# A hybrid mixer and MoE kernel: ten pieces of three weight blocks are loaded in the last tile of the RWKV recurrence

## The chip, the cores and the metric

The kernel runs on one core of a Trainium2 chip. The metric is the device time of one execution in microseconds (us). Times are medians of several runs; beside them stands one execution taken by the hardware profiler. The engines are TensorE (PE; its weight loads are listed as PEld), VectorE (DVE), ScalarE (ACT), GpSimd (POOL) and SyncE (SP), whose queue issues all the loads and stores here.

## The reference

One layer of a diffusion backbone over 256 latent tokens and 256 context tokens of width 1024. A modulated RMSNorm is followed by one input projection into three groups of heads: gated linear attention, RWKV-7 and Mamba-2 SSD. Each group is run in both directions, first over the context and then over the latent tokens from the context's last state. The three outputs are joined, projected and added to the input. Then comes a second modulated norm and a mixture of 32 experts, of which each token uses four:

```python
for e in range(N_EXPERTS):
    gu = t @ p['moe_w_gu'][e] + p['moe_b_gu'][e]
    glu, lin = jnp.split(gu, 2, axis=-1)
    glu = jnp.minimum(glu, SWIGLU_LIMIT)
    lin = jnp.clip(lin, -SWIGLU_LIMIT, SWIGLU_LIMIT)
    act = glu * jax.nn.sigmoid(SWIGLU_ALPHA * glu) * (lin + 1.0)
    y = y + gates[:, e:e + 1] * (act @ p['moe_w_down'][e] + p['moe_b_down'][e])
```

All is float32. The expert weights are 32 x 12 MB (12.6 million bytes each), by far the largest part of what is read.

## The kernel before

Everything on the chip lies in one SBUF arena of 57248 words per partition, and tensors of different stages share places in it. The stages are: modulation, norm and input projection with the GLA and SSD heads (to about 250 us of the profiled execution), the RWKV recurrence (to 367.5 us), the output projection, router and selection of tokens (to about 398 us), and the expert loop.

**Weight blocks and the ring.** An expert's weights are six blocks of 128 partitions x 4096 words (2.097 MB each): four of gate and up (s = 0 to 3) and two of down (s = 4, 5). They are read in order, expert by expert. The buffers are `ring[0]` to `ring[7]`; block number q of the whole sequence goes to ring q % 8, once TensorE has read the block that was in it (`ring_free[r]`, raised by TensorE after the last matmul on it). TensorE waits for `ring_full[r]`. Three further buffers, `ring[8]` to `ring[10]` (`RING`, `RING + 1`, `RING + 2`), are used once: they hold blocks 4, 5 and 3 of expert 20 (`AHEAD * GROUP`), loaded long before they are read. Two blocks, ring 4 (expert 0, block 4) and ring 6 (expert 1, block 0), lie where the output projection's weights and the residual stream are, and wait for these.

**The recurrence.** Four tiles of 128 tokens (s = 0 to 3), two directions each (d = 0, 1), in one chain through TensorE (`double`, `solve`, `transitions`, `updates`, `advance`, `outputs`), with DVE and ScalarE copying the products out of PSUM. Each tile has 6 doublings per direction, so there are 48 "rounds", named D{j}{s}{d}. Its working tensors (XT, Z, bt, AR, bm) have two halves, and tile s uses half s % 2. The third tile is s = 2 and so uses half 0; its last uses come in the first part of the last tile, s = 3, where TensorE's code has `solve(2)` (product qg2), `transitions(2)` (mt2), `updates(2)` (nv2) and later `outputs(2)` (ol2). The product `ro` ends the recurrence.

**Loads during the recurrence.** On the sync queue the loads are issued one part at a time (512 words per partition, 0.262 MB): `at_round(n)` makes the queue wait for round n's product, and `load_block_part(r, x)` issues part x of 8. In the last tile (rounds 36 to 47) these are the second half of ring 10 and the eight parts of ring 1 (issue line 681). The parts other than the eighth of a block raise `block_parts`, for which TensorE waits ahead of the expert loop (line 2977); the eighth raises `ring_full`. After `ro` the queue issues four whole blocks (`load_slot`, issue line 665): ring 3, 7, 8 and 9, which lie over the recurrence's working tensors; then the biases moe_b_gu (two rows of loads, line 716) and moe_b_down (line 717), which raise `late_in`, for which TensorE waits in `gates_by_expert`. Then come ring 4, ring 6, and from q = 8 on one block for each ring that comes free.

A semaphore table (`Rounds`) gives for each product the counts at which it is there (`Q.arrived`) and at which its PSUM bank has been read (`Q.emptied`).

Of the kernel before, what the change touches and what calls it, by code (L numbers as in the profile page):

```python
# [20 lines left out]
WORDS = 57248  # L21
RING = 8
PER = 6
GROUP = 4
AHEAD = 5
# [187 lines left out]
def rwkv_round_table():  # L213

    t = []

    def both(name, bank, parts=1):
        t.extend((f"{name}{d}", bank(d), parts) for d in (0, 1))

    doubling = lambda d: 2 * d  # L220
    lower, upper = (lambda d: 4 + 2 * d), (lambda d: 5 + 2 * d)

    def prepare(s, part):
        if part == 0:
            both(f"cu{s}", upper)
        if part == 1:
            both(f"ab{s}", lower)
        if part == 2:
            both(f"ak{s}", lower)
        if part == 3:  # L230
            both(f"bk{s}", lower)
            both(f"at{s}", upper)
        if part == 4:
            both(f"bv{s}", lower)

    def conclude(s, part):
        if part == 0:
            both(f"qg{s}", lower)
        if part == 1:
            both(f"mt{s}", lower)  # L240
        if part == 2:
            both(f"nv{s}", lower)
        if part == 3 and s > 0:
            both(f"rs{2 * s}", lower)
        if part == 4 and s < 3:
            both(f"rs{2 * s + 1}", lower)
        if part == 5 and s >= 2:
            both(f"ol{s}", lower)

    for part in range(4):  # L250
        prepare(0, part)
    for s in range(4):
        for j in range(DOUBLINGS):
            both(f"D{j}{s}", doubling, 2)
        if s < 3:
            prepare(s + 1, 0)
        prepare(s, 4)
        if s:
            for part in range(5):
                conclude(s - 1, part)  # L260
        if s < 3:
            prepare(s + 1, 1)
            prepare(s + 1, 2)
            prepare(s + 1, 3)
        else:
            conclude(2, 5)
    for part in (0, 1, 2, 3, 5):
        conclude(3, part)
    t.append(("ro", 0, 2))
    return t  # L270


def hybrid_block(nc, a):

    with ExitStack() as ctx:
# [109 lines left out]
        XT = [low.take(2, 4, 192) for _ in range(2)]  # L385
        XT = [XT[d].rearrange("p i (u m) (x t) -> p i u m x t", u=2, x=3) for d in range(2)]
        PLAIN, TURNED, SERIES = 0, 1, 2
        bm = [low.take(4, 64) for _ in range(2)]
# [15 lines left out]
        Z = [ra.take(8, 2, 64) for _ in range(2)]  # L404
        Z = [Z[d].rearrange("p (i o) x k -> p i o x k", i=2) for d in range(2)]
        bt = [ra.take(2, 2, 256) for _ in range(2)]
        AR = [ra.take(4, 2, 128) for _ in range(2)]
        AR = [AR[d].rearrange("p (i c) x (q t) -> p i c q x t", i=2, q=2) for d in range(2)]
# [4 lines left out]
        for x in (w0b, csil):  # L413
            room = over(x, 768)
            guarded, negative = room.take(2, 2, 65), room.take(2, P)
            d = len(eb)
# [51 lines left out]
        ring = [arena[:, ap.offset:ap.offset + 4096] for ap in ring_start] + held + [first_blocks[3]]  # L468
# [7 lines left out]
        Q = Rounds(rwkv_round_table(), bank_full, bank_free)  # L476
# [7 lines left out]
        ring_full = [sem(f"ring_full{r}") for r in range(RING + 3)]  # L484
# [14 lines left out]
        block_parts, out_parts = named("block_parts out_parts")  # L499
# [107 lines left out]
        gu_k = a["moe_w_gu"][0].rearrange("e (j p i) c -> e j p (i c)", p=P, i=2)  # L607
        dn_k = a["moe_w_down"][0].rearrange("e (j p i) c -> e j p (i c)", p=P, i=4)
# [12 lines left out]
        def extra_at(j, s):  # L621

            return s, j + (E * PER // RING - (1 if s in (3, 4, 5) else 0))
# [4 lines left out]
        def _(sp):  # L628
# [21 lines left out]
            for s, _, kind, n in loads[2 * KD + 2:]:  # L650
                if (kind, n) == ("in", 2):
                    sp.dma_start(Cb(1, C_N - 1), a["consts"][:, P:]).then_inc(consts_in, 16)
                if kind == "in":
                    size = KD * width_of(n)
                    slot_wait("in", n)
                    sp.dma_start(w_in_tile(n).rearrange("p k c -> p (k c)"), a["w_in"][w_in_at[n]:w_in_at[n] + P * size].rearrange("(p x) -> p x", p=P))\
                        .then_inc(slot_full[s], 16)
                elif kind == "ada":
                    load_ada(n)
            sp.dma_start(xT, a["xT"]).then_inc(xT_in, 16)  # L660

            def load_slot(r, e, s):

                src = gu_k[bass.ds(e, 1), s, :, :] if s < 4 else dn_k[bass.ds(e, 1), s - 4, :, :]
                sp.dma_start(ring[r], src.rearrange("a p c -> p (a c)")).then_inc(ring_full[r], 16)
# [7 lines left out]
            for n in range(2):  # L673
                s = place["out", n][0]
                slot_wait("out", n)
                sp.dma_start(slots[s], a["w_out"][n]).then_inc(slot_full[s], 16)
            def load_block_part(r, x):

                at = slice(512 * x, 512 * x + 512)
                src = gu_k[AHEAD * GROUP:AHEAD * GROUP + 1, 3, :, :] if r >= RING else gu_k[0:1, r, :, :] if r < 4 else dn_k[0:1, r - 4, :, :]  # L680
                sp.dma_start(ring[r][:, at], src.rearrange("a p c -> p (a c)")[:, at]).then_inc(ring_full[r] if x == 7 else block_parts, 16)

            def at_round(n):

                Q.arrived(sp, f"D{n % 12 // 2}{n // 12}{n % 2}")
# [16 lines left out]
            for x in range(8):  # L702
                at_round(28 + x)
                load_block_part(5, x)
            for x in range(4):
                at_round(36 + x)
                load_block_part(RING + 2, 4 + x)
            sp.wait_ge(slot_free[7], 1)
            for x in range(8):
                at_round(40 + x)  # L710
                load_block_part(1, x)
            Q.arrived(sp, "ro")
            for r, e, s in ((3, 0, 3), (7, 1, 1), (RING, AHEAD * GROUP, 4), (RING + 1, AHEAD * GROUP, 5)):
                load_slot(r, e, s)
            for x in range(2):
                sp.dma_start(bgrow[32 * x:32 * x + E, :], a["moe_b_gu"][0, :, FF * x:FF * x + FF]).then_inc(late_in, 16)
            sp.dma_start(bdn[BD, 0:D], a["moe_b_down"][0]).then_inc(late_in, 16)
# [8 lines left out]
            for q in range(RING, PER * GROUP):  # L726
                r, used = q % RING, q // RING
# [20 lines left out]
            with sp.If(extra > 0):  # L748
                with sp.Fori(0, extra) as j:
                    e = sp.value_load(ints[0:1, bass.ds(j + 8, 1)], min_val=0, max_val=E - 1)  # L750
                    for s in range(PER):
                        r, used = extra_at(j, s)
# [99 lines left out]
        def _(act):  # L852
# [45 lines left out]
            def conv_end(name):  # L898
                dst, _, n = conv[name]
                R.emptied(act, name)  # L900
                act.activation(dst, dst, ACT.Silu).then_inc(conv_silu, 1)
# [135 lines left out]
            def decays(s, d):  # L1037

                name = f"cu{s}{d}"
                Q.arrived(act, name)  # L1040
                if s:
                    act.wait_ge(rw_in, 2 * (s - 1) + d + 1)
                positive, negative, _, _ = eb[d]
                step(act.activation(positive, bank(name, 256).rearrange("p (c q t) -> p c q t", c=2, q=2), ACT.Exp))
                Q.drained(name, act.activation(negative, bank(name, 256).rearrange("p (c t) -> p c t", c=2), ACT.Exp, scale=-1.0))
# [207 lines left out]
        def _(dve):  # L1253
# [344 lines left out]
            def scale_by_decays(s, d):  # L1598

                cols, t = tile_cols(s, d), tile_of(s, d)  # L1600
                by_chunk = lambda ap: ap.rearrange("p c (q t) -> p c q t", q=2)
                _, EM, EX, whole = eb[d]
                Q.emptied(dve, f"cu{s}{d}")
                if s:
                    Q.arrived(dve, f"ak{s - 1}{d}")
                    dve.wait_ge(hats_ready, 4 * (s - 1) + 2 * d + 2)
                if s >= 2:
                    Q.arrived(dve, f"at{s - 2}{d}")
                step(dve.tensor_tensor(AR[d][:, s % 2, :, :, 0, :], by_chunk(kk[:, :, cols]), EX, ALU.mult))
                step(dve.scalar_tensor_tensor(out=be[d], in0=ba[:, :, cols], scalar=-1.0, in1=EM, op0=ALU.mult, op1=ALU.mult))  # L1610
                step(dve.tensor_copy(wc[d][:, :, 2 * t:2 * t + 2], whole[:, :, :, 64 - 64 * d]))
# [352 lines left out]
        def _(pe):  # L1964
# [697 lines left out]
            for tt in (2, 3):  # L2662
                for q in range(2):
                    for c in range(2):
                        at = L * c + P * (tt - 2) + 64 * q
                        for d in range(2):
                            s = TILE_ORDER[d].index(tt)
# [281 lines left out]
            def gates_by_expert():  # L2949

                R.claim(pe, "gt")
                pe.wait_ge(mask_ready, 2)
                for t in range(2):
                    mm(bank_of("gt")[0:96, 256:257], msk3[:, t, :], C[:, C_ONE, 0:1], start=t == 0, stop=t == 1)
                pe.wait_ge(late_in, 48)
                pe.wait_ge(gates_ready, 1)
                for t in range(2):
                    ins = mm(bank_of("gt")[BD, t * P:t * P + P], gates[:, t, :], ident, skip=True)
                R.filled("gt", ins)
# [14 lines left out]
            keep_warm(6, 1)  # L2974
            R.emptied(pe, "pos")
            gates_by_expert()
            pe.wait_ge(block_parts, 16 * 35)
            pe.wait_ge(sel_ready, 4)
            gather(0, 0)
            R.emptied(pe, "m5")  # L2980
# [92 lines left out]
```

## Time and profile before

| | us |
|---|---|
| median of 3 runs | 1309.31 (1308.84 to 1309.52) |
| the profiled execution | 1311.81 |
| its span in the trace | 1309.90 |
| TensorE busy | 1242.3 (95%) |
| DVE busy | 402.6 (31%) |
| ScalarE busy | 261.3 (20%) |
| GpSimd busy | 52.6 (4%) |

The page lists these queues (packets, MB, share of 16 DMA engines over the span):

```profile
q1 hardware_dynamic: 41328, 454.96, 83.4%
q8 instruction: 64, 1.05, 0.3%
```

The view of busy time by stretch has these columns: from and to in us, its length, busy time of PE, PEld, DVE, ACT and POOL with the number of instructions, the granted clock of TensorE (1.00 is 2.4 GHz), the mean busy share of the 16 DMA engines (a little over 1 where packets overlap), and GB/s moved. The chain of waits is followed back from the last instruction; "issue" in it is time in which the engine waited for nothing that the profile shows. L1968 is the line of the helper that issues nearly all matmuls.

### The profile page before, as it was taken

Reading aid. Unit: us, or ns where it says so; the run is one execution under the profiler, and the core shown is the slowest. Engines: PE = TensorE matmul, PEld = TensorE weight load, DVE = VectorE, ACT = ScalarE, POOL = GpSimd, SP = SyncE. Lnnn points to the kernel's source line nnn. Section 1 sums busy time; section 2 is a strip of 40 time slices with the busy share of each in tenths; the row PEclk is TensorE's granted clock in tenths of the full one; section 3 lists DMA queues with packets and bytes.
Section 4 is the critical chain, followed back from the end, with each engine's and each line's share of the span. In section 5 each row is a group of like instructions: output and inputs, shape, how many; then the busy total and the mean of one; then the engine's idle time right before and its main releaser. Section 6 shows DMA issues by size and latency. Waiting matters only on the chain.

```text
span 1309.9 us, 22318 instructions
## 1 busy us (share of the span) xinstructions
PE 1242.3 (95%) x9530; PEld 590.0 (45%) x9530; DVE 402.6 (31%) x906; ACT 261.3 (20%) x601; POOL 52.6 (4%) x89
## 2 busy tenths in 40 slices
PE   9999899889899999999999999998999999999987
PEld 6564665788784333333333333333333333333333
DVE  2466866655352111311122121111122121221112
ACT  3242238443332100101011001000111100110101
POOL 0014100311100000000000000000000000000000
PEclk9999999999999999999999999999999999999999
DMA  9954610343379999999999999999999999999995
GB/s 379 400 193 159 251 49 1 124 123 106 108 292 389 430 428 427 428 429 427 429 428 429 428 429 429 428 428 428 429 427 427 428 427 428 426 429 426 429 426 227
DMA packets 41406, 456.12 MB, mean 348 GB/s; under 512 B 4624, under 2 KB 4880, under 8 KB 12912
## 3 DMA queue, kind: packets, MB, share of 16 engines
q1 hardware_dynamic: 41328, 454.96, 83.4%
q8 instruction: 64, 1.05, 0.3%
q14 instruction: 14, 0.11, 0.0%
HBM read 453.89 MB, written 1.05 MB: 347 GB/s over the span
## 4 chain that ended last, share of the span: by engine, by line
PE 65%; DMA 26%; DVE 6%; issue 2%; ACT 1%; SPq 0%; DVEq 0%
PE PS L1968 61%; DMA arena<-in_moe_w_gu 24%; DMA arena<-in_moe_b_down 2%; DVE arena L1341 1%; PE PS L2864 1%; DVE arena L1861 1%; PE PS L1982 1%; DVE arena L1867 1%; DVE arena L1864 1%; PE PS L2855 1%; DVE arena L1860 0%; PE PS L2459 0%; DVE arena L1290 0%; ACT arena L894 0%; DVE arena L1249 0%
## 5 line engine op out<-in xcount | busy, mean ns | idle before, releaser
L1968 PE MATMUL PS<-arena 128*64 128x512 f32 (+11 forms) x9174 | 1197.3, 402 | 49.5 <-DMA arena<-in_moe_w_gu 25.5
L1968 PEld LDWEIGHTS PS<-arena 64*64 64x64 f32 (+5 forms) x9174 | 551.0, 145 | 645.2 <-issue 523.3
L1860 DVE TENSOR_SCALAR arena<-PS 128x256 f32<-128x256 f32 x64 | 38.8, 606 | 503.5 <-PE PS L1968 503.5
L1173 ACT ACTIVATE arena<-arena 128x256 f32<-128x256 f32 x64 | 26.7, 417 | 508.0 <-DVE arena L1860 508.0
L1889 DVE TENSOR_TENSOR arena<-PS,arena 128x512 f32<-128x512 f32 x32 | 22.2, 693 | 213.2 <-PE PS L1968 213.2
L1183 ACT COPY arena<-PS 128x256 f32<-128x256 f32 x32 | 11.9, 372 | 246.6 <-PE PS L2855 246.6
L1164 ACT ACTIVATE arena<-PS,arena 128x128 f32<-128x128 f32 x128 | 48.1, 456 | 35.4 <-PE PS L1968 35.4
L1626 DVE COPY arena<-PS 128x384 f32<-128x384 f32 (+2 forms) x48 | 23.4, 490 | 54.4 <-PE PS L1968 53.9
L1861 DVE TENSOR_SCALAR arena<-PS 128x256 f32<-128x256 f32 x64 | 39.3, 615 | 0.0
L1341 DVE SCALAR_TENSOR_TENSOR arena<-PS,arena 128x255 f32<-128x255 f32 (+5 forms) x68 | 32.6, 481 | 18.3 <-ACT arena L975 14.0
L1290 DVE SCALAR_TENSOR_TENSOR arena<-arena 128x2048 f32<-128x2048 f32 x14 | 33.2, 2369 | 7.6 <-DMA arena<-in_ada 7.5
L2864 PE MATMUL PS<-arena 128*128 128x128 f32 x128 | 26.4, 288 | 7.9 <-DVE arena L1867 7.9
L1086 ACT COPY arena<-PS 128x384 f32<-128x384 f32 (+2 forms) x48 | 20.4, 426 | 60.0 <-PE PS L1968 59.9
L2864 PEld LDWEIGHTS PS<-arena 128*128 128x128 f32 x128 | 14.2, 141 | 35.3 <-DVE arena L1867 24.4
L1864 DVE SCALAR_TENSOR_TENSOR arena<-arena 128x256 f32<-128x256 f32 x64 | 27.2, 425 | 3.9
L1867 DVE TENSOR_TENSOR arena<-arena 128x256 f32<-128x256 f32 x64 | 27.2, 426 | 2.2
L1178 ACT COPY arena<-PS 128x256 f32<-128x256 f32 x64 | 23.6, 369 | 6.0 <-PE PS L2864 6.0
L1836 DVE TENSOR_SCALAR arena<-arena 128x128 f32<-128x128 f32 x64 | 19.2, 343 | 0.2 <-issue 0.2
L2855 PEld LDWEIGHTS PS<-arena 128*128 128x128 f32 x64 | 6.5, 141 | 25.6 <-issue 25.6
L1823 DVE TENSOR_SCALAR arena<-arena 128x64 f32<-128x64 f32 x64 | 15.7, 309 | 2.8 <-PE PS L1968 2.8
L785 POOL TENSOR_TENSOR arena<-arena 128x128 f32<-128x128 f32 x8 | 10.8, 1350 | 112.9 <-ACT arena L933 84.6
L1982 PE MATMUL PS<-arena 128*128 128x128 f32 x78 | 11.6, 318 | 3.1 <-DMA arena<-in_consts 3.1
(262 smaller groups left out, 400.5 us busy)
## 6 DMA issues: line engine op xcount, KB each, us to landing
arena<-in_moe_w_gu SPq DMA_DIRECT2D x124, 2048.0 KB, 28.4
arena<-in_moe_w_down SPq DMA_DIRECT2D x63, 2048.0 KB, 30.1
arena<-in_ada SPq DMA_DIRECT2D x24, 1024.0 KB, 8.5
arena<-in_w_in SPq DMA_DIRECT2D x4, 2048.0 KB, 9.4
arena<-in_moe_w_gu SPq DMA_DIRECT2D x32, 256.0 KB, 3.1
arena<-in_opened SPq DMA_DIRECT2D x8, 576.0 KB, 17.7
arena<-in_tokens SPq DMA_DIRECT2D x4, 512.0 KB, 5.2
arena<-in_w_out SPq DMA_DIRECT2D x2, 1024.0 KB, 5.7
```

The costliest lines, as they stand in the source:

```text
L1164: ins = act.activation(hg[:, buffer, k, :], PS[:, bank, P * j:P * j + P], ACT.Identity, bias=scales[:, 1, k:k + 1], scale=scales[:, 0, k:k ...
L1173: act.activation(sgm[:, 256 * half:256 * half + 256], glu[:, 256 * half:256 * half + 256], ACT.Sigmoid, scale=ALPHA).then_inc(sig_ready, 1)
L1178: act.copy(actT[:, 2 * half:2 * half + 2].rearrange("p a b c -> p (a b c)"), src).then_inc(actT_ready, 1)
L1290: ins = dve.scalar_tensor_tensor(out=flat, in0=slots[sl], scalar=by_row, in1=flat, op0=ALU.mult, op1=ALU.add)
L1341: ins = dve.scalar_tensor_tensor(out=d_, in0=s_, scalar=wgt, in1=d_, op0=ALU.mult, op1=ALU.add)
L1860: dve.tensor_scalar(by_rest(glu), of_half(0), LIMIT, None, ALU.min).then_inc(glu_ready, 1)
L1861: dve.tensor_scalar(by_rest(lin), of_half(1), LIMIT, -LIMIT, ALU.min, ALU.max).then_inc(moe_vec, 1)
L1864: dve.scalar_tensor_tensor(out=lin[:, cols], in0=lin[:, cols], scalar=1.0, in1=glu[:, cols], op0=ALU.add, op1=ALU.mult).then_inc(moe_vec, 1)
L1867: dve.tensor_tensor(act_[:, cols], lin[:, cols], sgm[:, cols], ALU.mult).then_inc(act_ready, 1)
L1968: ins = pe.matmul(out, lhsT, rhs, start=start, stop=stop, skip_group_check=skip)
L1982: pe.matmul(PS[:, 0, 0:P], ident, ident, start=True, stop=True)
L2864: ins = pe.transpose(dst[:, c * P:c * P + P], act_[:, (2 * half + c) * P:(2 * half + c + 1) * P], ident)
```

## The change

The sync queue issues ten pieces of rings 3, 8 and 9 between the parts of ring 1 in the last tile, each over a half-0 tensor of the third tile: two pieces of 768 words over XT, two of 512 over Z, two of 512 over bt, two of 256 over bm and two of 512 over AR. Ahead of some of them it waits for a product that shows that the tensor has been read. After `ro` it issues ring 7 whole as before, and the rest of rings 3, 8 and 9 in ten pieces. Seven of the pieces after `ro` and the ten before it raise `block_parts`, and TensorE's count for it is raised from 35 to 52. Nothing else changes.

```diff
--- before.py
+++ after.py
@@ -702,6 +702,19 @@
             for x in range(8):
                 at_round(28 + x)
                 load_block_part(5, x)
+            held_at = {3: (0, 3), 7: (1, 1), RING: (AHEAD * GROUP, 4), RING + 1: (AHEAD * GROUP, 5)}
+
+            def load_piece(r, lo, hi, last=False):
+
+                e, q = held_at[r]
+                src = gu_k[e:e + 1, q, :, :] if q < 4 else dn_k[e:e + 1, q - 4, :, :]
+                sp.dma_start(ring[r][:, lo:hi], src.rearrange("a p c -> p (a c)")[:, lo:hi]).then_inc(ring_full[r] if last else block_parts, 16)
+
+            def piece_over(r, ap, words):
+
+                lo = ap.offset % WORDS - ring[r].offset % WORDS
+                load_piece(r, lo, lo + words)
+
             for x in range(4):
                 at_round(36 + x)
                 load_block_part(RING + 2, 4 + x)
@@ -709,9 +722,33 @@
             for x in range(8):
                 at_round(40 + x)
                 load_block_part(1, x)
+                d = x % 2
+                if x // 2 == 0:
+                    Q.arrived(sp, f"qg2{d}")
+                    piece_over(3, XT[d][:, 0], 768)
+                if x // 2 == 1:
+                    piece_over(RING, Z[d][:, 0], 512)
+                if x // 2 == 2:
+                    Q.arrived(sp, f"mt2{d}")
+                    Q.arrived(sp, f"nv2{d}")
+                    piece_over((RING, RING + 1)[d], bt[d][:, 0], 512)
+                if x // 2 == 3:
+                    Q.arrived(sp, f"bv3{d}")
+                    piece_over(3, bm[d], 256)
+                    Q.emptied(sp, f"ol2{d}")
+                    piece_over(RING + 1, AR[d][:, 0], 512)
             Q.arrived(sp, "ro")
-            for r, e, s in ((3, 0, 3), (7, 1, 1), (RING, AHEAD * GROUP, 4), (RING + 1, AHEAD * GROUP, 5)):
-                load_slot(r, e, s)
+            load_piece(3, 768, 1536)
+            load_piece(3, 2304, 3072)
+            load_piece(3, 3584, 4096, True)
+            load_slot(7, 1, 1)
+            load_piece(RING, 0, 1536)
+            load_piece(RING, 2048, 2560)
+            load_piece(RING, 3072, 3584, True)
+            load_piece(RING + 1, 0, 512)
+            load_piece(RING + 1, 1024, 1536)
+            load_piece(RING + 1, 2048, 2560)
+            load_piece(RING + 1, 3072, 4096, True)
             for x in range(2):
                 sp.dma_start(bgrow[32 * x:32 * x + E, :], a["moe_b_gu"][0, :, FF * x:FF * x + FF]).then_inc(late_in, 16)
             sp.dma_start(bdn[BD, 0:D], a["moe_b_down"][0]).then_inc(late_in, 16)
@@ -2974,7 +3011,7 @@
             keep_warm(6, 1)
             R.emptied(pe, "pos")
             gates_by_expert()
-            pe.wait_ge(block_parts, 16 * 35)
+            pe.wait_ge(block_parts, 16 * 52)
             pe.wait_ge(sel_ready, 4)
             gather(0, 0)
             R.emptied(pe, "m5")
```

## Rows read from the trace of the kernel before

**Rows 1.** The page: what DMA moved in 40 slices of the span, and the chain's shares.

```profile
GB/s 379 400 193 159 251 49 1 124 123 106 108 292 389 430 428 427 428 429 427 429 428 429 428 429 429 428 428 428 429 427 427 428 427 428 426 429 426 429 426 227
...
PE 65%; DMA 26%; DVE 6%; issue 2%; ACT 1%; SPq 0%; DVEq 0%
```

**Rows 2.** The chain of waits after 365 us: start us, us, what.

```profile
370.56 23.41 DMA arena<-in_moe_b_down
...
1242.33 33.47 DMA arena<-in_moe_w_gu
...
1275.84 9.77 PE PS L1968 x80
```

**Rows 3.** Busy time by stretch, 400 to 470 us; the last two columns are DMA's.

```profile
400.00:401.30 1.30, 1.30 (x8) 0.43 (x6) 0.00 (x0) 0.00 (x0) 0.00 (x0) 1.00 0.83 353
...
401.30:403.00 1.70, 1.70 (x10) 0.57 (x8) 0.00 (x0) 0.00 (x0) 0.00 (x0) 1.00 0.12 48
...
423.00:425.00 2.00, 2.00 (x12) 0.71 (x10) 0.00 (x0) 0.00 (x0) 0.00 (x0) 1.00 0.92 328
...
430.00:470.00 40.00, 40.00 (x196) 14.02 (x194) 6.53 (x18) 3.35 (x9) 0.00 (x0) 1.00 1.01 429
```

**Rows 4.** The same view, two stretches of one expert's length.

```profile
457.00:484.00 27.00, 26.84 (x138) 9.87 (x136) 5.04 (x12) 3.24 (x9) 0.00 (x0) 1.00 1.01 427
...
754.00:781.00 27.00, 24.86 (x124) 8.84 (x124) 6.02 (x16) 3.23 (x9) 0.00 (x0) 1.00 1.01 428
```

**Rows 5.** The sync queue's issues in order of time: start us, us, engine, line, what.

```profile
342.80 12.40 SPq L681 DMA_DIRECT2D arena<-in_moe_w_gu  x8
...
367.51 0.80 SPq L665 DMA_DIRECT2D arena<-in_moe_w_gu  x2
...
370.56 0.44 SPq L717 DMA_DIRECT2D arena<-in_moe_b_down  x1
...
383.44 0.35 SPq L665 DMA_DIRECT2D arena<-in_moe_w_down  x1
...
387.35 0.35 SPq L665 DMA_DIRECT2D arena<-in_moe_w_gu  x1
...
402.03 0.33 SPq L665 DMA_DIRECT2D arena<-in_moe_w_gu  x1
...
421.98 0.33 SPq L665 DMA_DIRECT2D arena<-in_moe_w_gu  x1
```

**Rows 6.** TensorE in order of time ahead of and in expert 0.

```profile
394.01 1.38 PE L1968 MATMUL PS<-arena 128*32 128x128 f32 x9 [0.48 <-DMA arena<-in_moe_b_down]
...
398.33 8.11 PE L1968 MATMUL PS<-arena 128*64 128x512 f32 x40
```

**Rows 7.** The chain of waits in the recurrence, pieces of kind issue.

```profile
263.99 2.13 issue
...
321.70 0.68 issue
...
347.32 1.97 issue
...
351.48 1.71 issue
```

**Rows 8.** Busy time by stretch around those pieces and after them.

```profile
263.50:266.20 2.70, 0.57 (x31) 0.43 (x27) 0.82 (x3) 1.15 (x3) 0.00 (x0) 1.00 0.55 175
...
319.90:322.40 2.50, 1.82 (x90) 1.69 (x90) 1.63 (x5) 0.37 (x1) 0.00 (x0) 1.00 0.80 284
...
342.80:355.00 12.20, 8.20 (x376) 7.72 (x376) 4.58 (x14) 2.57 (x7) 4.16 (x5) 1.00 0.39 120
...
346.50:349.30 2.80, 0.83 (x48) 0.70 (x39) 1.02 (x4) 0.49 (x2) 0.73 (x1) 1.00 0.77 237
...
350.40:353.20 2.80, 1.09 (x69) 0.99 (x63) 0.00 (x0) 0.00 (x0) 0.00 (x0) 1.00 0.03 6
...
355.90:359.70 3.80, 3.53 (x47) 3.39 (x44) 0.19 (x1) 1.15 (x2) 0.00 (x0) 0.57 0.35 119
```

## The prediction

> **What bounds the kernel now.** I began with the page: its slices show 427 to 430 GB/s from about 420 us on, and the chain of waits divides the span into 65% TensorE and 26% DMA [rows 1]. The chain's own pieces say where the DMA share lies: late, long pieces that wait for a gate-up block, the last of them just before the last expert's first matmuls [rows 2]. So I compared the two rates of the expert loop. One expert's six blocks are 6 x 2.097 MB; at 429 GB/s [rows 3] a block is 4.89 us and an expert 29.3 us. TensorE needs about 27 us for an expert while blocks lie ready (26.84 busy of 27.00), and shows gaps as soon as they don't (24.86 of 27.00) [rows 4]. The stream of blocks is the slower one, TensorE starts with a store of loaded blocks, and once the store is used up the stream sets the time. The end of the kernel is therefore: the moment from which the stream never pauses, plus the bytes left, plus a tail.
>
> What matters is that moment, and it is not the 367.5 us at which the four blocks of the change are issued. Around 402 us the stream pauses: 353 GB/s to 401.3, then 48 GB/s to 403 [rows 3]. The queue's issues say why. After slots 4 and 6 (383.44 and 387.35 us) nothing is issued until 402.03 [rows 5]: all buffers are full, and block eight waits until TensorE has read ring 0 in expert 0, whose matmuls began at 398.33 [rows 6]. A second, smaller pause is at 423 to 425 (328 GB/s) [rows 3], after the block issued at 421.98 [rows 5] had waited for ring 4. From there on it is full. Check: 192 blocks less the 11 loaded before 402 and the 4 issued before 421.98 are 177; 177 x 4.89 = 865.5, and 421.98 + about 1.3 (the 402.03 issue is followed by data at about 403.3) + 865.5 = 1289 us, which fits a last expert whose matmuls start at 1275.84, when its first block is in [rows 2]. So the end is tied to the start of expert 0 on TensorE, and not to when the blocks before it land.
>
> **The change part by part.** *Bytes moved forward.* The ten pieces are 2 x (768 + 512 + 512 + 256 + 512) = 5120 words per partition, 2.62 MB, 6.1 us of the stream. They leave 11264 words (5.77 MB, 13.5 us) and the biases to be loaded after the recurrence, where 8.39 MB (19.6 us) stood. By that the queue would be through with slot 6 not at 401.3 but at about 395. Nothing can follow it: the next issue still waits for ring 0. The pause of about 2 us grows to about 8 us, and the 6.1 us are spent as idle DMA. Worth to the end: 0.
>
> *The wait for the biases.* One wait of TensorE for DMA stands ahead of expert 0: 0.48 us for the row of moe_b_down before the matmuls at 394.01 [rows 6], which the chain shows as the 23.41 us piece from its issue at 370.56 [rows 2]. With 6.1 us fewer bytes ahead of it, that row lands at about 388 us and the wait goes. What is late next is nothing of DMA: the same group of matmuls waits for the gates, which are earlier in the record, and TensorE is busy from 394.01 to expert 0. Gain 0.48 us; bounds 0 (another releaser is only just ahead) and 0.48 (the whole wait). Later blocks are issued on TensorE's releases and all come earlier by the same 0.48.
>
> *Issues on the sync queue.* Ten more in the recurrence and seven more after it. One costs 0.33 us when alone and 0.40 in a series (0.80 for two) [rows 5]. After the recurrence 7 x 0.40 = 2.8 us puts the last bias issue at about 373.4 instead of 370.56; the backlog in front of it is 13.5 us, and slot 4 is not issued before 383.44. Cost 0. In the recurrence the eight issues of block 1 go from 342.80 over 12.40 us [rows 5]; ten more add 10 x 0.33 = 3.3 us, which fits before 367.51.
>
> *The added waits on the sync queue* (qg, mt, nv, bv of tile 3 filled, ol of tile 3 emptied). Behind each of them stand only the rest of block 1's parts and the wait for ro. By the order of TensorE's code the products of the first four are made in the first two or three doublings, up to round 41; outputs(2) stands between rounds 44 and 45, so its banks are emptied at about the time of rounds 46 and 47, whose issues end today at 355.2. Block 1's last part may be issued 1 us later; it is read by expert 0 after 402. Cost 0; if the cover went, the part would have to be over 40 us late. TensorE's raised count (52 parts) is met by the third piece of ring 9, at about 367.5 + 13 = 381 us, and TensorE asks at about 395. Cost 0.
>
> *The added traffic beside the recurrence.* This is the one part that can cost. The recurrence is a chain through TensorE, and every us in it moves expert 0 and with it the end. In it TensorE sometimes stops with nothing to wait for ("issue"): 2.13 us at 263.99, 0.68 at 321.70, 1.97 at 347.32, 1.71 at 351.48 [rows 7]. No operand is late in them, and the page lists 64 packets of 16 KB on a queue of kind "instruction". I take the stops for TensorE running out of fetched instructions. The fetch shares the DMA engines with the pieces, so more traffic may delay it. Today the stretch 342.80 to 355.00 has a DMA share of 0.39; 1.57 MB more until round 44 brings it, by 1.57 MB / 429 = 3.7 us over 12.2, to about 0.69, and the stretch of the stall at 351.48, which is empty now (share 0.03), will be under load. That of the stall at 347.32 already has 0.77 [rows 8]. What does load do to a stall? The loaded ones are 2.13 (share 0.55), 0.68 (0.80) and 1.97 (0.77), the unloaded one 1.71 (0.03): no order. Bounds for this stall: 0.68 - 1.71 = -1.0, and 2.13 - 1.71 = +0.42. I take +0.26, its loaded neighbour in the same code (1.97 - 1.71). The upper bound for the sum is a new stall of the size of the longest at the fetch after it, +2.1.
>
> The Trainium skill ("Runtime: NRT & Kernel Launch", Instruction fetch mechanics) says that the sequencer fetches blocks of 16 KiB through its own DMA queue and that crossing a boundary is mostly hidden. The packet size agrees with the trace; "mostly hidden" does not hold for the doublings, where 1.97 us stood open. By the page the traffic would cost nothing and the sum would be -0.48 instead of the one below.
>
> *DVE, ScalarE, GpSimd:* no instruction of theirs changes. TensorE has the same instructions and one other constant.
>
> **Sum.** 0 (bytes) - 0.48 (bias wait) + 0.26 (fetch under load) = -0.22 us. The profiled execution took 1311.81 us with a span of 1309.90 (1.91 outside it); it becomes about 1311.6. The median of the runs, 1309.31, is 2.5 us below the profiled execution; the same difference put on it gives **1309.1 us**.
>
> **Rivals.**
>
> *A. The stream was the bound from 367.5 us on.* Then the 2.62 MB taken out of it come back at the end: 1309.31 - 6.1 = 1303.2. For it: the slices of the page look full from there, the DMA waits late in the chain, and the stream does set the end. Against it: the pause at 401.3 to 403 and issues that wait for ring 0 [rows 3, 5]. It would need expert 0 to start earlier by 6 us, and TensorE is the one that is busy ahead of it. Chance 0.05.
>
> *B. Fetch stalls and TensorE's clock.* Slower. Place: 347 to 362 us. Under the pieces the stall at 347.32 grows to the longest seen (+0.16), that at 351.48 too (+0.42), and the fetch after them, which found TensorE slow enough to hide it, opens a stall of its own (the unloaded size, 1.71). Behind the stalls of today TensorE has a granted clock of 0.57 in 355.90 to 359.70 [rows 8], between 1.2 and 2.4 GHz and nearly all at the lower; a second such stretch costs 3.8 x (1 - 0.57) = 1.6. Together 3.9 - 0.48 = +3.4: 1312.7. It decides once the third fetch is late by more than its cover. For it: two stalls in a row already, and a fall of the clock after them. Against it: load and stall length have no order in the rows, and two-KB rows are short packets to wait behind. Chance 0.09.
>
> *C. The pieces do nothing at all* (the bias wait is replaced by the next thing, no stall moves): 1309.3. It lies in the forecast's own bin and can't be told from it. With the forecast 0.86.
>
> **How the numbers follow.** About 0.2% (2.6 us) is what a measurement of this kernel tells from no change. The forecast and C are within it: 0.86, with their bounds -1.0 - 0.48 = -1.5 to -0.48 + 2.1 = +1.6, that is 1307.8 to 1310.9, and this holds about 8 in 10, so it is the range given. Faster has A, 0.05; slower has B, 0.09.
>
> **What would show it.** Right: in the trace after, the DMA share from about 396 us to the next issue near 402 is near nothing, about 8 us long; the wait for moe_b_down is gone; expert 0 starts within 1 us of 398.3, the issue after slot 6 stays within 1 us of 402.03, and the sync queue shows ten more loads between 342.8 and 356. The first half of the fetch step is right if the stall near 351.5 is 1.7 to 2.2 us. Wrong: expert 0's first matmul before 396 or the issue on ring 0 before 400 (A); TensorE's "issue" idle between 345 and 367 above 5 us, or a second stretch of low clock (B). If the time falls by more than 1.5 us with expert 0 unmoved, the account of what ties the end is wrong.

## The result, and the profile after

The changed kernel takes 1313.01 us (median of 8 runs, 1310.61 to 1319.04), the kernel before 1309.37 (8 runs, 1308.42 to 1311.15): ratio 1.0029, 95% interval 1.0016 to 1.0043. It is slower, by 3.6 us at the median. The forecast was 1309.1, range 1307.8 to 1310.9: wrong, and the time that came is near rival B's (1312.7).

The profiled execution took 1314.23 us with a span of 1312.3 (before: 1311.81 and 1309.90). The page's transfers and the chain answer to [rows 1]:

```profile
GB/s 378 399 193 151 248 59 0 107 140 108 166 268 343 430 428 425 429 429 425 429 428 428 429 427 428 429 427 429 428 427 427 427 428 428 426 428 427 428 427 214
...
PE 66%; DMA 25%; DVE 5%; issue 2%; ACT 2%; SPq 0%; DVEq 0%
```

The eleventh slice holds more (166 for 108), the thirteenth less (343 for 389): the bytes moved forward. The stream after it is the same. The chain of waits in the last tile, against [rows 7]; the first row is the long piece of matmuls before the first stop:

```profile
329.43 17.86 PE PS L2005 x560
347.30 4.12 issue
...
355.11 0.58 issue
...
364.32 1.18 issue
```

Up to 347.30 the two executions agree to 0.02 us. Then the stop that was 1.97 is 4.12 us, and a third one, of 1.18, stands at 364.32, where the kernel before had 0.18. Busy time by stretch (columns as in the table before; the last three are TensorE's clock, DMA share and GB/s), against [rows 8] and [rows 3]:

```profile
342.80:355.00 12.20, 8.08 (x322) 7.94 (x323) 3.15 (x9) 1.81 (x4) 4.16 (x5) 0.86 0.76 239
344.00:347.00 3.00, 3.00 (x147) 3.00 (x143) 2.52 (x8) 1.30 (x3) 2.82 (x4) 1.00 0.95 237
...
348.00:351.00 3.00, 0.00 (x0) 0.00 (x0) 0.00 (x0) 0.00 (x0) 0.00 (x0) 1.00 1.03 391
351.50:354.30 2.80, 2.80 (x102) 2.80 (x106) 0.00 (x0) 0.00 (x0) 0.00 (x0) 0.50 0.57 214
...
400.00:403.00 3.00, 3.00 (x16) 1.00 (x14) 0.83 (x4) 1.35 (x4) 0.00 (x0) 1.00 0.03 11
403.00:404.30 1.30, 1.30 (x8) 0.43 (x6) 0.00 (x0) 0.00 (x0) 0.00 (x0) 1.00 0.00 0
```

From 348 to 351 no engine executes anything while the DMA engines are full; then TensorE runs at the lower clock. From 400 to 404.3 the DMA engines are idle, as forecast. What a DMA engine did for TensorE's instructions is in the transfers of one window, 344 to 348.5 us. Before:

```profile
q1 hardware_dynamic: 541, 0.99, 69.3%
q8 instruction: 1, 0.02, 1.4%
```

After, the same window and the next one, 348.5 to 352:

```profile
q1 hardware_dynamic: 474, 1.07, 94.4%
...
q1 hardware_dynamic: 724, 1.38, 103.0%
q8 instruction: 1, 0.02, 1.8%
```

The one packet of 16 KB of instructions that was read in the first window before comes only in the second after. Its start is at 346.84 and at 348.98 us, 2.1 apart; the ends of the two stops, 349.29 and 351.42, are as far apart.

That this packet ends the stop is seen in every trace of this document, fourteen in all. The last instruction packet ahead of the first stop's end is through 1.2 to 1.7 us before TensorE goes on, whether the stop took 0.33 us or 4.12, and it is the same for the second stop and the third. The stops also have a fixed place: 4491 matmuls stand ahead of the first one in the whole program and 4618 ahead of the second, in all thirteen traces but that of run 6. The 127 between them are seen in the kernel before as

```profile
349.29 2.19 PE L1968 MATMUL PS<-arena 64*64 64x64 f32 x127 [1.97 <-issue]
```

(the chain's row for the same stretch counts 119, since it leaves some out). TensorE's program is the same before and after but for one constant, so the change didn't shift them.

TensorE ahead of and in expert 0, and the sync queue, against [rows 6] and [rows 5]:

```profile
393.65 14.19 PE L2005 MATMUL PS<-arena 128*128 128x128 f32 x92 [0.50 <-ACT arena L1188]
```
```profile
376.04 1.95 SPq L753 DMA_DIRECT2D arena<-in_moe_b_gu  x2
378.03 0.42 SPq L754 DMA_DIRECT2D arena<-in_moe_b_down  x1
...
403.43 0.33 SPq L665 DMA_DIRECT2D arena<-in_moe_w_gu  x1
```

No wait for DMA stands there any more. The account of this pair: the first issue behind ro comes at 369.46 instead of 367.51 (+1.95), the bias wait goes (-0.48), so ring 0 is reissued at 403.43 instead of 402.03 (+1.40). From that issue to the end it is 908.9 us instead of 907.9. Beside that 1.0 us stands TensorE's clock in the last experts, which fell for a while here (1.00 in 1250 to 1275 in the kernel before):

```profile
1262.00:1275.00 13.00, 11.25 (x48) 3.77 (x46) 4.07 (x11) 1.39 (x4) 0.00 (x0) 0.87 1.00 427
```

Whether that belongs to the change isn't shown. The kernel of the third experiment, which is the kernel before but for the place of one block's load, shows it too (0.93 in 1250 to 1275). The second profile of the change (run 8b) has 1.00 in this place but 0.93 in 1225 to 1250, and there it is 909.7 us from ring 0's issue to the end; the second profile of before has 907.8.

### The profile page after: what moved, and what is told of

It is laid out like the page before. It is cut to its first block, busy times and chain, and to the rows that moved or that the text cites. A ratio compares the mean times of both kernels' runs of the same rounds, so it can differ in the third digit from the quotient of the medians.

```text
span 1312.3 us, 22337 instructions
## 1 busy us (share of the span) xinstructions
PE 1244.4 (95%) x9530; PEld 589.5 (45%) x9530; DVE 402.2 (31%) x906; ACT 261.5 (20%) x601; POOL 52.6 (4%) x89
## 4 chain that ended last, share of the span: by engine, by line
PE 66%; DMA 25%; DVE 5%; issue 2%; ACT 2%; SPq 0%; DVEq 0%
PE PS L2005 63%; DMA arena<-in_moe_w_gu 24%; PE PS L2901 1%; DMA arena<-in_opened 1%; DVE arena L1898 1%; DVE arena L1378 1%; DVE arena L1901 1%; DVE arena L1904 1%; PE PS L2892 1%; DVE arena L1897 0%; PE PS L2496 0%; ACT arena L931 0%; DVE arena L1998 0%; DVE arena L1327 0%; ACT arena L1025 0%
## 5 line engine op out<-in xcount | busy, mean ns | idle before, releaser
L2901 PEld LDWEIGHTS PS<-arena 128*128 128x128 f32 x128 | 14.2, 141 | 35.2 <-DVE arena L1904 24.4
```

The lines of the kernel that those rows point to most:

```text
L2901: ins = pe.transpose(dst[:, c * P:c * P + P], act_[:, (2 * half + c) * P:(2 * half + c + 1) * P], ident)
```

## The experiments

Times of the runs are medians; ratios are to the kernel before on the same chip. "Last tile" is from the start of the long piece near 329 us to the first issue behind ro, in one profile.

**1. The waits and cuts without the early loads.** Ten pieces issued after ro.

```diff
-                load_piece(r, lo, lo + words)
+                later.append((r, lo, lo + words))
+            for piece in later:      # behind Q.arrived(sp, "ro")
+                load_piece(*piece)
```

> The change with its waits and issues in place, but the ten pieces themselves issued after ro, ahead of the rest of their blocks. Theory F (fetch): TensorE runs out of fetched instructions in the doublings, and the pieces' traffic between 343 and 351 us delays the fetch; without it the stall near 347.3 us is 2.0 us again as before (4.12 in the change) and the time is that of before, 1309.4 (1308.5 to 1310.3). Theory W (the sync queue's waits, or the blocks cut into pieces after ro): as slow as the change, about 1313.

1313.4 us, 1.0031 (1.0019 to 1.0043): the time speaks for W. The trace divides it. Its stops are 1.38, 1.71 and 0.42 and its last tile is 37.6 us, 2.4 shorter than the change's, so F's part holds. But the biases are issued at 381.72 and TensorE waits for them:

```profile
394.26 3.10 PE L2009 MATMUL PS<-arena 128*32 128x128 f32 x15 [1.65 <-DMA arena<-in_moe_b_down]
```

After that wait it runs 4 us at half clock (0.50 at 396 to 398): 14.06 us for the work of 12.43. So this kernel pays 1.2 + 1.6 us behind the tile, and it doesn't separate waits from cuts. Runs 9 and 10 do.

**2. The pieces in one go behind round 47.** As 1, with the loop ahead of `Q.arrived(sp, "ro")`.

> The change with all ten pieces issued in one go after the last part of ring 1, behind round 47 (about 355 us). F: the stalls near 347.3 and 351.5 us are 2.0 and 1.7 us as before; the traffic now lies over the fetches after 356, where TensorE issues fewer instructions, and costs 0 to 1.2 us there (the change has a stall of 1.18 at 364.3): 1309.0 to 1310.6. Theory B (any 2.6 MB more in the last tile cost the same): 1313.

1314.6 us, 1.0048 (1.0034 to 1.0062). The first two stops are small (1.06 and 1.16), and a long one stands where the pieces now are:

```profile
359.40 3.37 issue
```

The last tile is 39.8 us. F's mechanism moved with the load, but my price for the later place (0 to 1.2) was far too low: the time expected was at most 1310.6.

**3. Ring 1 held back to round 47, in the kernel before.**

```diff
+            at_round(47)
             for x in range(8):
-                at_round(40 + x)
                 load_block_part(1, x)
```

> The kernel before with the eight parts of ring 1 held back to round 47 and then issued together; no other edit. F: from 343 to 355 us nothing but ring 10's last part moves; the page of instructions then takes 3.9 us from entry, as where no load runs, so the stall near 347.3 falls from 1.97 to about 0.6, that at 351.5 stays 1.7 and comes 1.4 earlier; the burst of 2.1 MB after 354 can cost up to 1 us of it again: 1308.0 to 1309.4. If stalls don't depend on load: 1309.4 and a stall of 2.0.

1315.0 us, 1.0043 (1.0030 to 1.0056), where 1308.0 to 1309.4 was expected. The first two stops are as expected, the third is long as in run 2; the clock in 341 to 368 is 0.83. Last tile 40.8 us. This kernel loads not a byte more than the one before, it loads them in one burst. Of the 5.2 us by which its tile is longer than in the second profile of before (run 8a), the stops are 1.9, and most of the rest is time at half clock.

```profile
328.32 17.86 PE PS L1968 x561
346.19 0.51 issue
348.89 1.69 issue
360.34 2.61 issue
```

**4. No load in the last tile.**

```diff
             sp.wait_ge(slot_free[7], 1)
             Q.arrived(sp, "ro")
+            for x in range(4):
+                load_block_part(RING + 2, 4 + x)
+            for x in range(8):
+                load_block_part(1, x)
```

> The kernel before with no load at all in the last tile: ring 10's second half and ring 1 are issued after ro. For its stalls, not its time. F: last tile's stalls 0.6 and 1.7 us, ro about 1.4 us earlier. The time is worse all the same: 3.1 MB (7.3 us) more stand ahead of the biases, so that expert 0 starts about 6 us later: about 1315. If stalls don't depend on load, 2.0 and 1.7.

Stops 0.33 and 1.71, last tile 34.8 us, the first issue behind ro 3.0 us earlier than in the first profile of before (the 35.2 in the expectation of run 5 is read from the second issue). The time is 1321.5 (2 runs; expected about 1315), with a wait of 8.8 us for the biases, where I had expert 0 about 6 us later.

```profile
347.53 0.33 issue
350.06 1.71 issue
```

**5. Ring 1 after ro, biases first.** The kernel before with the parts of ring 1 deleted from the tile; behind ro come the three bias loads, `load_slot(1, 0, 1)`, then the four blocks.

> The kernel before with ring 1 taken out of the last tile: after ro the queue issues the biases first, then ring 1 whole, then the four blocks as before. Theory F (in-tile loads delay TensorE's instruction fetch): the last tile, from the start of its long piece near 329.5 to ro, takes about 35.5 us (35.2 with no load at all, 38.1 before), no wait for the biases (0.48 before), so ring 0 is free and reissued about 3 us earlier, at 399.5 to 400. The queue is then through with slot 6 at about 401.7, so the stream of blocks begins about 1.6 us earlier than the 403.3 of before: 1307.7 (1306.8 to 1308.7). If in-tile loads cost nothing, the 2.1 MB more after ro make it 2 to 3 us slower: 1312.

1309.51 us, 0.9994 (0.9982 to 1.0006): no difference, the expected 1307.7 missed. Both things I expected of the queue came: no bias wait, and no pause of the stream at ring 0 (418 GB/s before, 442 and 410 after it). Stops 0.83, 1.71 and 0.34, but the last tile is 37.1 and not 35.5 us; its clock is 0.94. Ring 0 was reissued 1.7 us earlier than in the first profile of before, and that wasn't the bound here, because the queue was never empty. Between 368 and 400 us it moved 412 GB/s and not the 429 reckoned with, which is 1.3 us of its bytes, and at 410 us as much was left to load as before (377.1 and 376.9 MB). So the bytes moved behind ro took back what the shorter tile gave.

**6. TensorE's program shifted by 64 instructions.**

```diff
+            for _ in range(128):
+                pe.wait_ge(zeroed, 1)
             pe.wait_ge(ident_in, 16)
```

(Two waits make one instruction.)

> The kernel before with 64 more instructions at the head of TensorE's program, in its wait for the first load; no load is moved. F: TensorE stops where a fetched page of 256 instructions ends, so each stop in the doublings comes 64 instructions (about 30 matmuls) earlier in the program: the long piece of 564 matmuls before the stop at 347.3 becomes one of about 530, and the stops have other sizes; the time may change by up to 3 us either way. If the stops belong to a place in the code (a semaphore, a bank), the piece stays at about 564.

```profile
332.98 17.58 PE PS L1968 x522
350.56 1.63 issue
354.38 1.70 issue
```

The row of the chain has 522 matmuls instead of 564, but it leaves some out. Counted over the whole program, 4459 matmuls stand ahead of the first stop instead of 4491, and 4586 ahead of the second instead of 4618. Both came 32 matmuls earlier, which with their 32 weight loads are the 64 instructions added, and there are 127 between them again:

```profile
352.18 2.20 PE L1968 MATMUL PS<-arena 64*64 64x64 f32 x127 [1.63 <-issue]
```

The stops belong to the count of instructions and not to a place in the code. The time is 1315.0, 1.0033 (1.0018 to 1.0048), and its last tile begins 3.5 us later: the stages ahead of it pay for the shift. With no load moved this costs as much as the change does.

**7. Long rows.** The change with ring 1's part x as `ring[1][16x:16x+16, 0:4096]`.

> The change, with each of ring 1's eight parts in the last tile as 16 partitions x 4096 words instead of 128 partitions x 512: same bytes, same rounds, one eighth of the rows. If a fetch waits behind bytes: the stop near 347.3 stays at about 4 us and the time at 1313. If it waits behind rows: the rows in the tile fall from 1024 + 1280 to 128 + 1280, the stop to 2.5 to 3, the time to 1311.5.

1326.9 us, 1.0131 (1.0111 to 1.0152), which neither reading foresaw. The first stop, 2.53, is of the size given for rows; the second, of 7.62, fits neither.

```profile
346.21 2.53 issue
352.23 7.62 issue
370.35 3.43 issue
```

The transfers are slower too (184 GB/s at a share of 1.02 in 343 to 353), so the engines are full for longer, and the run doesn't tell bytes from rows.

**8a. The kernel before again.**

> The kernel before once more, for a second profile: how much its last tile (38.06 us from the start of the long piece to ro) and its stops (1.97 and 1.71) differ between executions of the same kernel. Kernels with the same loads up to round 44 showed 1.1 to 2.0 for the first of them.

```profile
328.95 17.87 PE PS L1968 x564
346.81 1.16 issue
350.16 1.44 issue
360.23 0.36 issue
```

Last tile 35.6 us, 2.5 less than in the profile on which the prediction was made: 0.7 by shorter stops, about 1.5 by the clock, which is 1.00 in 341 to 368 here and was 0.94 there. The profiled time is 1308.77, against 1311.81: that one lay above all of the first eight runs.

**8b. The change again.**

> The changed kernel once more, for a second profile. Theory F (in-tile loads delay TensorE's instruction fetch): its last tile, from the start of the long piece to ro, took 40.03 us; the kernel before took 38.06 (with a stretch at half clock) and 35.60 (without). F: again 39 to 41 us, first stop 3 to 4.5 us, no wait for the biases.

```profile
329.10 17.87 PE PS L2005 x563
346.97 3.25 issue
353.80 1.50 issue
363.94 1.72 issue
```

Last tile 41.8 us, a little over the 39 to 41 expected. The time is 1313.3 (10 runs; the kernel before on that chip 1310.3), the ratio 1.0016 (1.0006 to 1.0027): smaller than at first and still slower. The instruction packets behind the first stops start at 345.71 us in run 8a and 347.82 here, 2.1 apart as in the first pair.

**8. The pieces, without ring 1 in the tile.** The change, with ring 1 whole after ro.

```diff
                 at_round(40 + x)
-                load_block_part(1, x)
...
             Q.arrived(sp, "ro")
+            load_slot(1, 0, 1)
```

> The change with ring 1 not loaded in the last tile but whole right after ro; the ten pieces, their places and waits stay. In-tile bytes from round 40 on are 2.62 MB instead of 4.72 (before: 2.10). F: the stops depend on the traffic as a whole and not on the pieces: first stop 1 to 2 us, last tile 36 to 38 us, time 1309 to 1311. If the pieces as such cost (their waits, or that they are written into tensors still in use): 1313 as the change.

1311.33 us (the kernel before on that chip 1310.3), 1.0002 (0.9993 to 1.0011): no difference. Last tile 36.5 us.

```profile
344.78 0.50 issue
347.47 2.26 issue
359.03 0.41 issue
```

The pieces in their places, with their waits, cost nothing that can be measured (up to 1.4 us by the interval) when they replace other traffic (2.62 for 2.10 MB). What costs in the change is pieces and parts together.

**9. The waits alone,** put into the kernel before: ten waits at the places of the change (the expectation's "six" is a miscount).

> The kernel before with the change's six waits on the sync queue between the parts of ring 1, and nothing else. F: 1309.5 to 1310, no difference. If the waits hold up ring 1 and through it the queue: up to 1313, and the issues of its last two parts come later.

1309.9 us, 0.9991 (0.9980 to 1.0003). The waits cost nothing that can be measured.

**10. The cuts alone:** rings 3, 8 and 9 after ro in 7 + 6 + 7 pieces.

> The kernel before with rings 3, 8 and 9 after ro cut in the twenty pieces that the change makes of them (16 of them more than 7 loads in a row), and nothing else. Theory S: the cut blocks hold up the queue, the biases land about 1 us later than with whole blocks, TensorE waits for them 1.5 us and then runs a few us at half clock, as in the run with the pieces after ro (1.65 us and 1.6 us): 1312 to 1313.5. If the cuts cost nothing, that run's time came from its waits: 1309.6.

1312.14 us, 1.0014 (1.0004 to 1.0024), as S said, with a bias wait of 2.16 us:

```profile
390.96 4.28 PE L1983 MATMUL PS<-arena 128*32 128x128 f32 x35 [2.16 <-DMA arena<-in_moe_b_down]
```

In this profile, the fastest of its eleven runs, no fall of the clock followed. The cuts cost 1.8 us and the waits nothing, so run 1, which has both and is 4.1 us slower, pays for its cuts, and more than run 10 does; its stretch at half clock (1.6 us) is part of the rest. In the change itself half of the pieces have gone ahead, and the wait is gone.

The last tiles side by side (us; stops are pieces of kind issue over 0.3; clock is the granted mean in 341 to 368; the last column is the time of the profiled execution and, in brackets, the median of the kernel's runs, since one profile can be from either end of them):

| kernel | MB from round 40 to ro | stops | clock | last tile | profiled (median) |
|---|---|---|---|---|---|
| no loads (4) | 0 | 0.33, 1.71 | 1.00 | 34.8 | 1319.3 (1321.5) |
| ring 1 after ro (5) | 0 | 0.83, 1.71, 0.34 | 0.94 | 37.1 | 1312.1 (1309.5) |
| before, again | 2.10 | 1.16, 1.44, 0.36 | 1.00 | 35.6 | 1308.8 (1309.6) |
| before | 2.10 | 1.97, 1.71 | 0.94 | 38.1 | 1311.8 (1309.4) |
| before with waits (9) | 2.10 | 1.59, 1.71, 0.41 | 0.94 | 37.9 | 1314.1 (1309.9) |
| before with cuts (10) | 2.10 | 1.38, 1.44, 0.63 | 1.00 | 36.1 | 1308.9 (1312.1) |
| before, 64 instructions more (6) | 2.10 | 1.63, 1.70, 0.61 | 0.94 | 37.9 | 1315.0 (1315.0) |
| pieces after ro (1) | 2.10 | 1.38, 1.71, 0.42 | 0.94 | 37.6 | 1314.1 (1313.4) |
| pieces, no ring 1 (8) | 2.62 | 0.50, 2.26, 0.41 | 0.94 | 36.5 | 1307.3 (1311.3) |
| ring 1 behind round 47 (3) | 2.10 | 0.51, 1.69, 2.61 | 0.83 | 40.8 | 1315.0 (1315.0) |
| pieces behind round 47 (2) | 4.72 | 1.06, 1.16, 3.37 | 0.92 | 39.8 | 1314.4 (1314.6) |
| the change | 4.72 | 4.12, 0.58, 1.18 | 0.94 | 40.0 | 1314.2 (1313.0) |
| the change, again | 4.72 | 3.25, 1.50, 1.72 | 0.92 | 41.8 | 1316.5 (1313.3) |
| the change in long rows (7) | 4.72 | 2.53, 7.62, 3.43 | 0.75 | 51.6 | 1323.7 (1326.9) |

The share of busy DMA engines doesn't order the first stops: it was 0.84 just ahead of the 0.50 of run 8 and 0.79 ahead of the 4.12. What orders them better is what had been issued and not yet moved. I take the packet that ends the first stop, and how long after the one before it it started. With nothing outstanding 3.5 us after the packet before, that was 3.5 to 3.8 us (3 traces); with 0.2 to 0.5 MB outstanding 4.1 to 5.0 (8 traces); with 1.0 to 1.1 MB, the two profiles of the change, 7.4 and 6.7; with 1.2 MB in long rows 5.5. The bytes outstanding are an estimate, the loads issued less the packets through. The packets behind the long third stops of runs 2 and 3 fit in, with 1.3 and 0.8 MB and 7.2 and 8.1 us.

## Why the prediction was wrong, step by step

*What ties the end to expert 0 was right.* The queue ran dry before 400, the next issue came with ring 0's release, and the bytes moved forward became idle DMA: [rows 3] had 1.7 us of 0.12, after it is 4.3 us of about 0.02. The whole pause is 5.3 us, from about 399 to 404.3, and not the 8 foreseen, as the queue began 1.95 us later behind ro and moved less per us. From ring 0's issue to the end it took 907.8 to 909.8 us in all fourteen traces. Rival A is refuted. The check in the prediction came out by luck, though: it has the stream end at 1289 us, and its last weights landed at 1294.9, since it moved 426 GB/s in the mean and not 429. Nothing in the sum hangs on it.

*The bias wait was right:* 0.48 us before, none after. *The added waits* at 0 were right (run 9). *The issues after ro* at 0 held in the change, but with less cover than I gave: the last bias issue came at 378.03 and not at 373.4 (the seven issues of line 711 from 371.26 took 4.74 us, 0.68 each instead of 0.40), and with all the cuts and no bytes moved forward they cost 1.8 us (run 10).

*The step that failed is "the added traffic beside the recurrence", priced at +0.26 us.* The mechanism was the one named; the size was not, and its upper bound of +2.1 was too low as well. The last tile took 40.0 and 41.8 us in two profiles of the change and 38.1 and 35.6 in two of the kernel before: +4.1 in the mean, of which the stops are 2.9 (6.2 us in the mean for 3.3) and most of the rest is the clock. With -0.48 that is +3.6, as the medians have it (+3.6, and +3.0 in the second set of runs), but so close an agreement is luck: the four profiles differ by 5.0 us as a whole, because the stretch behind ring 0's issue is 1.4 longer in those of the change, and the two tiles of the same kernel are 2.5 apart. Three things went into the error.

First, I took the longest stop of the trace (2.13) as a bound. It was the longest of four, at DMA shares of 0.03 to 0.80. With 1.0 MB outstanding the instruction packet came 2.1 us later than before and the stop was 4.12, in the second profile 3.25. The rows of before held no such case, and I should have bounded by the bytes that would be outstanding instead of by the longest seen.

Second, I gave the extra bytes 429 GB/s. Rows 8 say otherwise: 237 GB/s at a share of 0.77, which is 308 at a full share. After, 344 to 347 moved 237 GB/s at 0.95. At that rate 2.62 MB fill the DMA engines for 11 us and not 6.1.

Third, I looked at the stop at 351.48, the one without load. It did not grow (0.58, 1.50). In the first profile of the change TensorE came to it at half clock, 3.70 us for the 127 matmuls instead of 2.19, and the packet had that much longer to come. The one at 347.3 did grow, which already had load and which I had left alone; and a third opened near 364, as rival B said.

Rival B named all that came, and its sign is there (the stops of the tile add up to 5.88 us, over the 5 it asked for). Still its total is near by luck: it had the first stop 0.16 longer (2.15 came), the second 0.42 longer (1.13 shorter), a third of 1.71 (1.18), and 1.6 us for a second stretch at half clock (the clock is 0.94 in both first profiles). I gave it 0.09, on the ground that load and length had no order in four rows at other places.

The pattern of a stop shows in the trace of before as well: from 349.29 to 351.48 TensorE did 127 matmuls, 254 instructions with their weight loads, between two stops, and with waits that is one packet of 16 KB. Where it runs through a packet in 2.2 us, the next is late even with no load (1.71 in run 4), for in no trace did a packet in or just ahead of this tile start less than 3.3 us after the one before; where traffic delays it, the whole delay is on the path. The Trainium skill ("Runtime: NRT & Kernel Launch", Instruction fetch mechanics) has blocks of 16 KiB with 256 instructions and calls the cost of crossing from one to the next "mostly hidden". The stops, 254 instructions and their waits apart, agree with the first. The second is not so here, where the first crossing with a stop in this tile cost 0.33 to 4.12 us.

Also unforeseen: the profile I argued from was an unlucky one. Its half-clock stretch of 3.8 us is most of the 2.5 us by which the kernel before looks slower in the last tile than in its second profile. A stretch of this kind follows some of the stops and not others (the clock is 0.83 in run 3 and 1.00 in run 10), which spreads the times of all these kernels.

What stays open: whether a fetch waits behind the outstanding bytes themselves or behind something that goes with them (run 7 changed rows, rate and fullness together, and no run set the outstanding bytes alone), why the tile's transfers run at 237 GB/s while TensorE works and at 391 while all engines stand still, and what decides whether the clock falls. The split of the 4.1 us into 2.9 of stops and the rest holds for these four profiles only; how the 3.6 us of the medians divide can't be said from two profiles each.

## What to carry to other kernels

Bytes moved ahead of a full stream gain nothing if the stream waits for a consumer: look for a pause of the transfers behind the place, and for the release that ends it. Where an engine issues short instructions without a break (here 254 in 2.2 us), its next instructions have to come over the same DMA engines as the data, so free DMA time beside such a stretch is not free. Here about the same amount spread out was neutral (run 8), more of it cost 3.6 us, and the same amount in one burst cost 5.6 (run 3). Count what is outstanding when a fetch is due. A longest case seen at light load is no bound for heavy load.

## What the runs showed of the hardware

- In the densest stretch TensorE stopped with no operand missing after 127 matmuls with their weight loads, in all fourteen traces; 64 more instructions at the program's head moved the stops 32 matmuls forward. Each stop of over 0.3 us in the last tile ended 1.2 to 1.7 us after the end of a packet of 16 KB on the instruction queue.
- The first such stop of the last tile took 0.33 to 0.83 us with no data outstanding, 0.50 to 1.97 with 0.2 to 0.5 MB of loads outstanding, and 3.25 and 4.12 with 1.0 to 1.1 MB (2.53 with 1.2 MB in long rows). The packet that ended it took 1.0 to 1.4 us itself in all of them; what differed was when it started.
- Parts of 128 rows of 2 KB moved 237 GB/s at a share of 0.95 while the engines worked, and 391 at 1.03 while none did. With ring 1's parts as 16 rows of 16 KB the tile's loads moved 184 at 1.02, with stops of 2.53, 7.62 and 3.43 us.
- The granted clock was 0.50 (1.2 GHz) for some 3 us after a stop of 4.12, and stayed 1.00 after stops of 1.16 and 1.44.
